# Two transformer-like blocks on one core: GpSimd takes the cosine products and the sister convolution tile, TensorE takes split sums of squares and picked gate rows

## The chip, the cores and the metric

One Trainium2 chip, one of its cores. The metric is the device time of one execution in microseconds (us); lower is better. Five engines work side by side: TensorE (PE; its weight loads are shown apart as PEld), VectorE (DVE), ScalarE (ACT), GpSimd (POOL) and SyncE (SP, which here issues the weight loads from memory).

## The reference

The program runs two blocks one behind the other, each with two layers (DEPTH = 2), on 512 tokens of width 1024, all in float32. What matters here:

```python
def first_block(x, ...):
    for i in range(DEPTH):
        h = rms_norm(x, attn_norm_g[i])
        proj = h @ w_in[i]
        q, k, v, u, vv = jnp.split(proj, split_at, axis=-1)
        q = rms_norm(q.reshape(b, s, N_HEADS, HEAD_DIM), q_norm_g[i])
        k = rms_norm(k.reshape(b, s, N_KV_HEADS, HEAD_DIM), k_norm_g[i])
        q = axial_rope(q, tables)          # q * cos - swapped(q) * sin
        k = axial_rope(k, tables)
        attn_o = gqa_attention(q, k, v)
        sg_o = spatial_gating(jax.nn.gelu(u), jax.nn.gelu(vv), ...)   # rms_norm over heads of 64 first
        ...
def second_block(x, ...):
    for i in range(DEPTH):
        z = rms_norm_2(x, attn_pre_norm[i]) @ w_in[i]
        aq, ak, av, conv_u, gdn_qkv, gdn_gate, gdn_a, gdn_b = jnp.split(z, offsets, axis=-1)
        y_attn = dilated_attention_mixer(aq, ak, av, positions)
        y_conv = conformer_conv_mixer(conv_u, ...)     # causal depthwise convolution, 31 taps, 256 channels
        y_gdn = gated_deltanet_mixer(gdn_qkv, ...)     # g: decay per token and head, beta: gate per token and head
        x = x + rms_norm_2(mix @ w_out[i], attn_post_norm[i])
        ...
```

In the delta rule the decay between two tokens of a chunk is exp(G[a] - G[b]), with G the running sum of g in the chunk.

## The kernel before

Activations lie transposed: features on 128 partitions, 512 tokens along the row. Every matrix product is made of **units**: one unit is an output tile of 128 features x 512 tokens. A weight tile of 8 x 128 x 128 is loaded into `raw`, ACT rounds it to fp32r (`whi`, `hi_next`, L1564), DVE makes the rest (`wlo = raw - whi`, `low`, L2276), and PE forms 24 products in fp32r (`whi` with `h_hi`, `whi` with `h_lo`, `wlo` with `h_hi`; L701). The weights are double buffered and units use two accumulator banks, `ACC`; unit i + 2 waits for the `low` that DVE issues in its own step i, and for the copy out of its bank. An ordinary float32 product on PE shows as two records in the trace.

Each engine's program is an unrolled list whose steps carry the number i of the unit: PE runs unit i and then small work of step i; ACT and DVE begin their step i when unit i is done. Engines meet only in semaphores, and nothing reorders an engine's queue.

**Block 1, input units (i = 0 to 13).** Tiles: v, k, four of q, four of vv, four of u. For k and q (j = 0 to 4), in DVE's steps: the copy out of the bank (L2377); then `qk_norm` (scale by the root of the mean square, L2331), `qk_rotary` (product with the sine table, a shuffle of lanes, product with the cosine table, subtraction; L2337 to L2343) and `qk_low`. ACT squares the tile into `msq` (`qk_square`), PE sums over the 64 features of a head with a float32 product with the block matrix `blk` (`head_sums`, L874, behind unit j + 2), and ACT takes log and exp of it (`qk_rs`). The four vv tiles go the same way behind units 10 and 11 (`gated_sums`, L883).

**Block 2, input units (i = 0 to 23, "input stage").** Beside them run the rotary of the four attention tiles (its sine part on POOL, L660), the scores of four heads (`scores`, L1127; DVE's `row_max`, L2666, must have read the bank before the next, semaphore `S_used`), `scores_turned` (L1142), `exponentials` on ACT, the products with counts on POOL (`counted`, L635), `probs_values` (L1164), the short convolutions of the delta rule (`short_taps`, L2687), and the 31-tap convolution of two tiles: taps 0 to 22 of both tiles on DVE (`taps`, L2710, in steps 9 to 20 by the list `beside`), the last 8 of tile 0 on DVE (`late_tap`, L2796), the last 8 of tile 1, the **sister tile**, as a product on ACT (`tap_product`, L2017) that POOL adds (L676).

The gates' running sums are made behind unit 20 (`decay_sums`). Behind units 20 to 23 PE runs `head_in(h)`, h = 0 to 3 (the text calls these steps heads 0 to 3; the trace shows them after the last products of units 20 to 23): a row of decays, broadcast to all partitions, by four products of a broadcast column of g with the triangle `tri` (L1197), the same for beta with the identity (L1203), then the transposes of k (L1210, waits for `turned_used`: ACT has read the former head's bank) and of v (L1214, waits for ACT's `short_silu`). ACT's `head_scaled(h)` uses them and ends with L1943.

**Levels.** Behind the units come 24 steps n of a blockwise inversion, with three groups of 16 short PE records each (`level_first` L1305, `level_second` L1327, `level_turned` L1348). ACT copies each turned result to `xd` (L2033, `xt_kept`); `level_first(n)` waits for the copy of step n - 4. ACT's late tap products stand in the same list, each waiting until POOL has freed one of two buffers.

## Time and profile before

| | |
|---|---|
| median of 3 runs | 2551.18 us (2549.28 to 2551.55) |
| the profiled execution, its own time | 2552.15 us |
| span of its instructions | 2550.4 us |
| mean granted TensorE clock | 0.995 |
| busy, share of the span | PE 98%, PEld 78%, DVE 61%, ACT 43%, POOL 9% |
| block 1's two input stages | about 36 to 116 us and 590 to 669 us |
| block 2's two input stages | about 1132 to 1347 us and 1837 to 2052 us |

The span is the time from the first to the last instruction; the execution's own time lies 1.75 us above it. A record of a pipelined product lasts longer than the distance to the next one, so the pace of products is read from their starts or ends, not from their durations. "Idle before" names who ended an engine's wait.

### The profile page before, as it was taken

How to read it: one execution, taken by the hardware profiler on the slowest of the kernel's cores; microseconds unless marked ns; L12 is line 12 of the kernel's file. 1: busy time of each engine (PE TensorE's matmuls, PEld its weight loads, DVE VectorE, ACT ScalarE, POOL GpSimd, SP SyncE). 2: the span in 40 equal slices, each digit the busy share in tenths (PEclk: the TensorE clock that was granted, in tenths of full speed). 3: DMA queues.
4: the chain of work that ended last, by engine and by line, in shares of the span. 5: the costliest groups of instructions: out<-in, count | busy, mean ns of one | idle time of the engine just before them, and what ended most of it. 6: DMA issues, size and time to landing. Idle time of an engine off the chain costs nothing.

```text
span 2550.4 us, 36617 instructions
## 1 busy us (share of the span) xinstructions
PE 2492.4 (98%) x12846; PEld 1992.5 (78%) x12856; DVE 1545.0 (61%) x1994; ACT 1094.3 (43%) x1597; POOL 227.2 (9%) x186
## 2 busy tenths in 40 slices
PE   7999999999999999999999999999999999999998
PEld 5768888887668888887688778888776887788886
DVE  5766755757666736647986554344579865643444
ACT  4655423435554424433485442233334754431323
POOL 1010000000000000004212020000142120200000
PEclk9999999999999999999999999999999999999999
DMA  4203332333113333342120223233222202233333
GB/s 134 78 17 91 95 109 84 100 98 88 58 42 99 97 96 96 103 111 74 50 75 11 66 83 107 86 96 97 80 72 58 67 19 65 77 107 90 96 97 95
DMA packets 384483, 208.07 MB, mean 82 GB/s; under 512 B 9866, under 2 KB 380500, under 8 KB 384372
## 3 DMA queue, kind: packets, MB, share of 16 engines
q1 hardware_dynamic: 381284, 202.79, 27.5%
q0 software_dynamic: 2176, 3.06, 0.6%
q8 instruction: 65, 1.06, 0.2%
q10 hardware_dynamic: 912, 0.77, 0.1%
q14 instruction: 46, 0.38, 0.0%
HBM read 205.34 MB, written 2.10 MB: 81 GB/s over the span
## 4 chain that ended last, share of the span: by engine, by line
PE 88%; DVE 7%; ACT 2%; issue 1%; DMA 0%; POOL 0%; DVEq 0%; SPq 0%; ACTq 0%; POOLq 0%
PE ps L701 64%; PE ps L720 6%; PE ps L986 2%; DVE yc L2710 1%; DVE wlo L2276 1%; ACT whi L1564 1%; PE ps L1305 1%; PE ps L1164 1%; PE ps L1046 1%; PE ps L1048 1%; PE ps L1047 1%; PE ps L1176 1%; PE ps L1426 1%; PE ps L1428 1%; PE ps L1427 1%
## 5 line engine op out<-in xcount | busy, mean ns | idle before, releaser
L1564 ACT ACTIVATE whi<-raw 128x1024 fp32r<-128x1024 f32 (+1 forms) x354 | 395.8, 1118 | 989.4 <-PE ps L701 844.2
L701 PE MATMUL ps<-h_hi,whi 128*128 128x512 f32 x1920 | 761.8, 397 | 2.3 <-DVE za L2616 1.7
L701 PE MATMUL ps<-h_lo,whi 128*128 128x512 f32 x1920 | 750.0, 391 | 0.0
L701 PE MATMUL ps<-h_hi,wlo 128*128 128x512 f32 x1920 | 513.3, 389 | 0.0
L2276 DVE TENSOR_TENSOR wlo<-raw,whi 128x1024 fp32r<-128x1024 f32 (+1 forms) x354 | 467.0, 1320 | 64.2 <-ACT whi L1564 63.0
L701 PEld LDWEIGHTS ps<-h_hi,whi 128*128 128x128 f32 x1920 | 362.2, 189 | 84.3 <-issue 4.2
L701 PEld LDWEIGHTS ps<-h_lo,whi 128*128 128x128 f32 x1920 | 362.1, 189 | 78.7 <-issue 4.3
L701 PEld LDWEIGHTS ps<-h_hi,wlo 128*128 128x128 f32 x1920 | 360.5, 188 | 74.9
L701 PE MATMUL ps<-a_hi,whi 128*128 128x512 f32 x592 | 230.3, 389 | 0.0
L701 PE MATMUL ps<-a_lo,whi 128*128 128x512 f32 x592 | 230.3, 389 | 0.0
L3039 DVE TENSOR_TENSOR cv<-ps,rstd 128x512 f32<-128x512 f32 x80 | 55.3, 692 | 228.7 <-PE ps L701 228.7
L701 PE MATMUL ps<-a_hi,wlo 128*128 128x512 f32 x592 | 152.4, 389 | 0.0
L2525 DVE TENSOR_TENSOR pad<-ps,rstd 128x512 f32<-128x512 f32 x88 | 61.0, 693 | 130.6 <-PE ps L701 118.4
L701 PEld LDWEIGHTS ps<-a_lo,whi 128*128 128x128 f32 x592 | 111.1, 188 | 23.1
L701 PEld LDWEIGHTS ps<-a_hi,wlo 128*128 128x128 f32 x592 | 111.1, 188 | 23.0
L701 PEld LDWEIGHTS ps<-a_hi,whi 128*128 128x128 f32 x592 | 111.1, 188 | 23.0
L2488 DVE TENSOR_TENSOR x_sb<-x_sb,ps 128x512 f32 (+1 forms) x40 | 27.5, 687 | 110.1 <-PE ps L701 94.2
L2534 DVE SCALAR_TENSOR_TENSOR cv<-pad,pc,cv 128x512 f32<-128x512 f32 x88 | 66.1, 751 | 11.0
L1815 ACT ACTIVATE cv<-pad,pc,pb 128x512 f32<-128x512 f32 x88 | 70.6, 802 | 0.1
L2965 DVE COPY y_sb<-ps 128x512 f32<-128x512 f32 (+1 forms) x24 | 16.6, 691 | 88.8 <-PE ps L701 66.6
L1827 ACT ACTIVATE a_hi<-prod 128x512 f32 (+1 forms) x44 | 27.9, 633 | 97.8 <-DVE prod L2541 97.8
L2710 DVE SCALAR_TENSOR_TENSOR yc<-ypad,pd,yc 128x512 f32<-128x512 f32 x88 | 68.5, 819 | 1.6
(429 smaller groups left out, 3427.0 us busy)
## 6 DMA issues: line engine op xcount, KB each, us to landing
raw<-in_w_up SPq DMA_DIRECT2D x128, 512.0 KB, 3.8
raw<-in_w_down SPq DMA_DIRECT2D x64, 704.0 KB, 4.5
raw<-in_w_in SPq DMA_DIRECT2D x82, 512.0 KB, 3.8
raw<-in_w_gate SPq DMA_DIRECT2D x40, 512.0 KB, 3.8
raw<-in_w_o SPq DMA_DIRECT2D x16, 512.0 KB, 3.6
raw<-in_w_out SPq DMA_DIRECT2D x16, 512.0 KB, 3.7
xs<-in_x SPq DMA_DIRECT2D x2, 1024.0 KB, 6.8
raw<-in_w_gate SPq DMA_DIRECT2D x8, 256.0 KB, 2.8
```

Of the source, the lines that this page charges most:

```text
L701: return pe.matmul(ps[:, ACC[s], :], w[s][:, k, :], r[:, k, :], start=start, stop=stop)
L720: return pe.matmul(ps[:, ACC[s], :], w[s][:, k, :], r[:, k, :], start=start, stop=stop)
L986: pe.matmul(ps[:, TRN[h % 2], :], vaug[:, h // GROUP, h % 2, kt, :], probs[:, kt, :], start=(kt == 0), stop=(kt == TB - 1)).then_inc(PV_do ...
L1564: act.activation(whi[s][:, 0:kt, :], raw[s][:, 0:kt, :], ACT.Copy).then_inc(w_hi_ready.sem, 1)
L1815: act.activation(cv[s][:], pad[s][:, 1:SEQ + 1], ACT.Identity, scale=param(pb, L, 2 * NF + col), bias=param(pc, L, 2 * NF + col))\
L1827: act.activation(tile(a_hi, j), prod[:], ACT.Copy).then_inc(ahi_ready.sem, 1)
L2276: dve.tensor_tensor(wlo[s][:, 0:kt, :], raw[s][:, 0:kt, :], whi[s][:, 0:kt, :].bitcast(F32), ALU.subtract).then_inc(w_lo_ready.sem, 1)
L2488: dve.tensor_tensor(tile(x, n), tile(x, n), ps[:, ACC[s], :], ALU.add).then_inc(acc_free.sem, 1)
L2525: dve.tensor_tensor(pad[s][:, 1:SEQ + 1], ps[:, ACC[s], :], rstd[:], ALU.mult).then_inc(acc_free.sem, 1)
L2534: dve.scalar_tensor_tensor(cv[s][:], pad[s][:, 2:SEQ + 2], param(pc, L, col), cv[s][:], ALU.mult, ALU.add)\
L2710: ins = dve.scalar_tensor_tensor(yc[:, t, :], src, w, yc[:, t, :], ALU.mult, ALU.add)
L3039: dve.tensor_tensor(cv[s][:], ps[:, ACC[s], :], rstd[:], ALU.mult).then_inc(acc_free.sem, 1)
```

## The change

1. **Sums of squares in two parts (block 1).** POOL rounds each square tile to fp32r (`sq_hi`) and takes the rest (`sq_lo`); PE sums both with `blk_r`, an fp32r copy of `blk`: two fp32r products in place of one float32 product, 9 tiles in each layer. The sums come one unit later (behind unit j + 3), in four banks instead of two; `qk_rs`, `qk_norm`, `qk_rotary`, `qk_low` and `qk_high` move one step later with them.
2. **Cosines on POOL (block 1).** POOL makes the product with the cosine table; DVE keeps sine product, shuffle and subtraction.
3. **Sister tile off DVE (block 2).** All 31 taps of tile 1 are products on ACT that POOL adds: by the table `SIDE`, taps 0 to 15 in steps 10 to 17, taps 16 to 19 in steps 18 to 21, taps 20 to 30 in the levels. DVE keeps tile 0.
4. **Picked gate rows (block 2).** `decay_sums` moves from behind unit 20 to behind unit 12. DVE splits the running sums and beta into fp32r parts (`gate_split`), PE turns them behind unit 13 (four transposes), DVE keeps the rows (`gate_rows`), and `head_in` picks a head's row with one fp32r product of 512 columns for the decays and one for beta, instead of four float32 products of 128 columns each.
5. Two unused tables are no longer loaded.

```diff
--- before.py
+++ after.py
+    SIDE = {**{10 + p: (2 * p, 2 * p + 1) for p in range(8)}, **{18 + n: (16 + n,) for n in range(4)}}
+    SIDE_IN = 20
...
+                def square_split(j):
+
+                    if j <= NQ:
+                        pool.wait_ge(qksq_ready.sem, qksq_ready.at(L, j))
+                    else:
+                        pool.wait_ge(vvsq_ready.sem, vvsq_ready.at(L, j - NQ - 1))
+                    if j >= 4:
+                        pool.wait_ge(qkstat_ready.sem, qkstat_ready.at(L, j - 4))
+                    square = msq[:, j % 2 if j <= NQ else (j - NQ - 1) % 2, :]
+                    nc.gpsimd.tensor_copy(sq_hi[:, j % 4, :], square).then_inc(sq_split.sem, 1)
+                    pool.wait_ge(sq_split.sem, sq_split.at(L, 2 * j))
+                    nc.gpsimd.tensor_tensor(sq_lo[:, j % 4, :], square, sq_hi[:, j % 4, :].bitcast(F32), ALU.subtract).then_inc(sq_split.sem, 1)
+                    pool.wait_ge(sq_split.sem, sq_split.at(L, 2 * j + 1))
+
+                def cosines(i):
+
+                    pool.wait_ge(qkn_ready.sem, qkn_ready.at(L, i))
+                    if i >= 2:
+                        pool.wait_ge(rope_ready.sem, rope_ready.at(L, i - 2))
+                    nc.gpsimd.tensor_tensor(probs[:, 2 + i % 2, :], zk[:] if i == 0 else zq[:, i - 1, :], rope[:, 0, :], ALU.mult)\
+                        .then_inc(cos_ready.sem, 1)
+                    pool.wait_ge(cos_ready.sem, cos_ready.at(L, i))
+
+                for j in range(NQ + 1):
+                    square_split(j)
+                    if j >= 2:
+                        cosines(j - 2)
+                for i in range(NQ - 1, NQ + 1):
+                    cosines(i)
...
+                    if h == 1:
+                        pool.wait_ge(qm_ready.sem, qm_ready.at(L, h))
+                        for j in range(NQ + 1, NQ + 1 + NS):
+                            square_split(j)
...
+                def side_tap(k):
+
+                    pool.wait_ge(tap_scaled.sem, tap_scaled.at(L, k))
+                    if k > 0:
+                        if k > 1:
+                            pool.wait_ge(late_tapped.sem, late_tapped.at(L, k - 2))
+                        nc.gpsimd.tensor_tensor(yc[:, 1, :], yc[:, 1, :], msq2[:, k % 2, :], ALU.add)\
+                            .then_inc((late_tapped if k < CT - 1 else dw_ready).sem, 1)
+
+                for i in range(10, 22):
+                    p = i - 10
+                    if p < 2 * AH:
+                        for kt in range(2 * (p % 2), 2 * (p % 2) + 2):
+                            counted(p // 2, kt)
+                    for k in SIDE[i]:
+                        side_tap(k)
...
-                for n in range(CT - TAPS_IN):
-                    pool.wait_ge(tap_scaled.sem, tap_scaled.at(L, n))
-                    if n >= 1:
-                        pool.wait_ge(late_tapped.sem, late_tapped.at(L, n - 1))
-                    nc.gpsimd.tensor_tensor(yc[:, 1, :], yc[:, 1, :], kb[:, n % 2, :], ALU.add)\
-                        .then_inc((late_tapped if n < CT - TAPS_IN - 1 else dw_ready).sem, 1)
+                for k in range(SIDE_IN, CT):
+                    side_tap(k)
...
-                def head_sums(i):
-
-                    pe.wait_ge(qksq_ready.sem, qksq_ready.at(L, i))
-                    if i == 0:
+                def square_sums(j):
+
+                    bank = ps[:, (STAT + ROT)[j % 4], :]
+                    pe.wait_ge(sq_split.sem, sq_split.at(L, 2 * j + 1))
+                    if j == 0:
                         pe.wait_ge(rstd_ready.sem, rstd_ready.at(L * 2, 0))
-                    if i >= 2:
-                        pe.wait_ge(qkrs_ready.sem, qkrs_ready.at(L, i - 2))
-                    pe.matmul(ps[:, STAT[i % 2], :], blk[:], msq[:, i % 2, :], start=True, stop=True).then_inc(qkstat_ready.sem, 1)
-
-                def gated_sums(t):
-
...
-                    pe.matmul(ps[:, STAT[t % 2], :], blk[:], msq[:, t % 2, :], start=True, stop=True).then_inc(vvstat_ready.sem, 1)
+                        pe.wait_ge(acc_free.sem, V * 2 + 3)
+                    if 4 <= j < NQ + 5:
+                        pe.wait_ge(qkrs_ready.sem, qkrs_ready.at(L, j - 4))
+                    pe.matmul(bank, blk_r[:], sq_hi[:, j % 4, :], start=True, stop=False)
+                    pe.matmul(bank, blk_r[:], sq_lo[:, j % 4, :], start=False, stop=True)\
+                        .then_inc((qkstat_ready if j <= NQ else vvstat_ready).sem, 1)
...
                     unit(V + i // 2, i % 2, KD, h_hi, h_lo, need_h(L * 2))
-                    if i - 2 <= NQ:
-                        head_sums(i - 2)
+                    if 0 <= i - 3 <= NQ:
+                        square_sums(i - 3)
                     if i == 4:
                         turn_spatial()
                     if i == 6:
                         turn_values()
                     if i in (10, 11):
-                        gated_sums(2 * i - 20)
-                        gated_sums(2 * i - 19)
+                        square_sums(NQ + 1 + 2 * i - 20)
+                        square_sums(NQ + 1 + 2 * i - 19)
...
+                def turn_gate_parts():
+
+                    pe.wait_ge(gate_parts.sem, gate_parts.at(L, 0))
+                    for tb in range(TB):
+                        mm = pe.transpose(ps[0:4 * GH, TRN[1], tb * P:(tb + 1) * P], gate_split[:, tb, :].bitcast(F32), ident[:])
+                    mm.then_inc(gate_turned.sem, 1)
...
-                        mm = pe.matmul(ps[:, ROT[0], tb * P:(tb + 1) * P], cols["g"][:, tb, h:h + 1].to_broadcast([P, P]),
-                                       tri[:], start=True, stop=True)
-                    mm.then_inc(grow_ready.sem, 1)
+                    n = 4 * GH
+                    pe.matmul(ps[:, ROT[0], :], gate_pick[0:n, h:h + 1].to_broadcast([n, P]), gate_rows[0:n, :],
+                              start=True, stop=True).then_inc(grow_ready.sem, 1)
                     if h >= 1:
                         pe.wait_ge(kb_ready.sem, kb_ready.at(L, h - 1))
-                    for tb in range(TB):
-                        mm = pe.matmul(ps[:, ROT[1], tb * P:(tb + 1) * P], cols["beta"][:, tb, h:h + 1].to_broadcast([P, P]),
-                                       ident[:], start=True, stop=True)
-                    mm.then_inc(brow_ready.sem, 1)
+                    pe.matmul(ps[:, ROT[1], :], gate_pick[0:n, GH + h:GH + h + 1].to_broadcast([n, P]), gate_rows[0:n, :],
+                              start=True, stop=True).then_inc(brow_ready.sem, 1)
...
+                    if i == 12:
+                        decay_sums()
+                    if i == 13:
+                        turn_gate_parts()
...
+                def tap_product(k):
+
+                    if k == 0:
+                        act.wait_ge(glu_ready.sem, glu_ready.at(L, 1))
+                        dst, bias = yc[:, 1, :], param(pd, L, D_BIAS + 1)
+                    else:
+                        dst, bias = msq2[:, k % 2, :], 0.0
+                    if k >= 3:
+                        act.wait_ge(late_tapped.sem, late_tapped.at(L, k - 3))
+                    order.told(act.activation(dst, ypad[:, 1, k:k + SEQ], ACT.Identity, bias=bias, scale=param(pd, L, D_DW + k * NC + 1)),
+                               tap_scaled, L, k)
...
+                    for k in SIDE.get(i, ()):
+                        tap_product(k)
...
-                    if n in (0, 1):
-                        act.wait_ge(kk_ready.sem, kk_ready.at(L, GH - 2 + n))
-                        tap_product(n)
-                    if 2 <= n - 2 < CT - TAPS_IN:
-                        act.wait_ge(late_tapped.sem, late_tapped.at(L, n - 4))
-                        tap_product(n - 2)
+                    if n < CT - SIDE_IN:
+                        tap_product(SIDE_IN + n)
...
-                    order.step(dve.tensor_tensor(t1[:], z, rope[:, 0, :], ALU.mult))
-                    order.settle()
-                    order.told(dve.tensor_tensor(z, t1[:], t2[:], ALU.subtract), rope_ready, L, i)
+                    dve.wait_ge(cos_ready.sem, cos_ready.at(L, i))
+                    order.told(dve.tensor_tensor(z, probs[:, 2 + i % 2, :], t2[:], ALU.subtract), rope_ready, L, i)
...
+                def decay_columns():
+
+                    dve.wait_ge(G_ready.sem, G_ready.at(L, 0))
+                    order.told(dve.tensor_copy(flat("gc"), ps[:, TRN[1], 0:NCOL]), gc_kept, L, 0)
+                    order.settle()
+                    order.told(dve.tensor_tensor(flat("dg"), ps[:, TRN[1], NCOL:2 * NCOL], flat("gc"), ALU.subtract), dg_ready, L, 0)
+                    for n, name in enumerate(("gc", "beta")):
+                        order.step(dve.tensor_copy(gate_split[:, :, 2 * n * GH:(2 * n + 1) * GH], cols[name][:]))
+                    order.settle()
+                    for n, name in enumerate(("gc", "beta")):
+                        hi, lo = (slice((2 * n + e) * GH, (2 * n + e + 1) * GH) for e in range(2))
+                        ins = dve.tensor_tensor(gate_split[:, :, lo], cols[name][:], gate_split[:, :, hi].bitcast(F32), ALU.subtract)
+                        if n == 0:
+                            order.step(ins)
+                        else:
+                            order.told(ins, gate_parts, L, 0)
...
+                        w, src = param(pd, L, D_DW + k * NC), ypad[:, 0, k:k + SEQ]
+                        if k == 0:
+                            ins = dve.tensor_scalar(yc[:, 0, :], src, w, param(pd, L, D_BIAS), ALU.mult, ALU.add)
+                        else:
+                            ins = dve.scalar_tensor_tensor(yc[:, 0, :], src, w, yc[:, 0, :], ALU.mult, ALU.add)
+                        order.step(ins)
...
+                    if i == 12:
+                        decay_columns()
+                    if i == 13:
+
+                        dve.wait_ge(gate_turned.sem, gate_turned.at(L, 0))
+                        order.told(dve.tensor_copy(gate_rows[0:4 * GH, :], ps[0:4 * GH, TRN[1], :]), rows_kept, L, 0)
```

On PE, at head 1 of block 2 (ps is PSUM; `tri` and `ident` are constants, `col_g` and `col_beta` the gates by token), the program before has:

```order
L1197 MATMUL ps<-tri,col_g 128x128 [waits eg_ready]
L1197 MATMUL ps<-tri,col_g 128x128 x3
L1203 MATMUL ps<-ident,col_beta 128x128 [waits kb_ready]
L1203 MATMUL ps<-ident,col_beta 128x128 x3
L1210 MATMUL ps<-ident,gk 128x128 [waits l2n,turned_used]
```

and the changed one, at the same place:

```order
L1253 MATMUL ps<-gate_rows,gate_pick 128x512 [waits eg_ready]
L1257 MATMUL ps<-gate_rows,gate_pick 128x512 [waits kb_ready]
L1263 MATMUL ps<-ident,gk 128x128 [waits l2n,turned_used]
L1263 MATMUL ps<-ident,gk 128x128 x3
L1267 MATMUL ps<-ident,gv 128x128 [waits sc_silu]
```

The eight short products have become two; the waits behind them stay as they were.

On ACT, at the start of the levels (`gk<-ps` is the copy to `xd`, `kb<-ypad` or `sqt<-ypad` a tap product; the semaphore that the tap products wait for is named after its first use and is POOL's count of added taps), before:

```order
L1948 ACTIVATE eg_last<-eg 128x4
L2017 ACTIVATE kb<-ypad,pd 128x512 [waits kk_ready] x2
L2033 ACTIVATE gk<-ps 128x256 [waits osq_ready] x3
L2017 ACTIVATE kb<-ypad,pd 128x512 [waits qkstat_ready]
L2033 ACTIVATE gk<-ps 128x256 [waits osq_ready]
```

and in the changed program:

```order
L2012 ACTIVATE eg_last<-eg 128x4
L1955 ACTIVATE sqt<-ypad,pd 128x512 [waits qkstat_ready] x2
L2094 ACTIVATE gk<-ps 128x256 [waits osq_ready]
L1955 ACTIVATE sqt<-ypad,pd 128x512 [waits qkstat_ready]
L2094 ACTIVATE gk<-ps 128x256 [waits osq_ready]
```

The first tap product that waits for POOL stood behind three copies and now stands behind one.

On POOL, in block 1's input stage, before, the queue went from the loads of tables straight to the query copies:

```order
L555 DMA sgb<-in_sg_b 64x4x128 x2
L564 COPY qm<-qab 64x512 [waits qr_ready] x2
L564 COPY qm<-qab 64x512 [waits ST_ready,qr_ready] x2
L574 TENSOR_TENSOR ssq<-sqt 128x512 [waits osq_ready,qm_ready]
L574 TENSOR_TENSOR ssq<-ssq,sqt 128x512 [waits osq_used,osq_ready] x2
```

and in the changed program splits and cosine products stand between them:

```order
L597 CAST sq_hi<-sqt 128x512 [waits qksq_ready,sq_split]
L599 TENSOR_TENSOR sq_lo<-sqt,sq_hi 128x512 [waits sq_split]
L607 TENSOR_TENSOR probs<-zk,rope 128x512 [waits qkn_ready,sq_split]
L597 CAST sq_hi<-sqt 128x512 [waits qksq_ready,cos_ready]
L599 TENSOR_TENSOR sq_lo<-sqt,sq_hi 128x512 [waits sq_split]
```

POOL's work here is 5 splits with 5 cosine products, and 4 more splits for vv behind the first two query copies.

## Rows read from the trace of the kernel before

**Rows 1.** The page: busy time, share of the span and instructions of each engine.

```profile
PE 2492.4 (98%) x12846; PEld 1992.5 (78%) x12856; DVE 1545.0 (61%) x1994; ACT 1094.3 (43%) x1597; POOL 227.2 (9%) x186
```

**Rows 2.** Waits of PE: who for whom, us in total, times, longest.

```profile
PE ps L1127 <- DVE mx L2666: 5.9, 3, 2.8
```

**Rows 3.** Timeline of PE around two square sums: start us, us, instruction, count.

```profile
89.75 1.75 PE L701 MATMUL ps<-h_hi,wlo 128*128 128x512 f32 x7
...
91.79 0.39 PE L701 MATMUL ps<-h_hi,wlo 128*128 128x512 f32 x1
92.02 1.88 PE L883 MATMUL ps<-sqt,blk 128*128 128x512 f32 x4
```

**Rows 4.** Timeline of PE, block 2, heads 0 and 1.

```profile
1313.24 1.05 PE L1197 MATMUL ps<-tri,col_g 128*128 128x128 f32 x8
1314.12 1.06 PE L1203 MATMUL ps<-ident,col_beta 128*128 128x128 f32 x8
1315.02 0.60 PE L1210 MATMUL ps<-ident,gk 128*128 128x128 f32 x4
1315.45 0.60 PE L1214 MATMUL ps<-ident,gv 128*128 128x128 f32 x4
...
1324.94 0.60 PE L1210 MATMUL ps<-ident,gk 128*128 128x128 f32 x4
```

**Rows 5.** Windows of block 2's step 11, of step 13, and layer 2's step 11.

```profile
core 0: us, PE busy (x) PEld busy (x) DVE busy (x) ACT busy (x) POOL busy (x), PEclk, DMA share, GB/s
1214.34:1228.24 13.90, 10.83 (x36) 8.12 (x37) 13.44 (x17) 3.31 (x8) 2.07 (x2) 0.75 0.14 38
1239.12:1246.88 7.76, 7.69 (x36) 6.11 (x37) 7.41 (x10) 1.84 (x4) 1.51 (x2) 1.00 0.24 67
1920.12:1932.50 12.38, 9.31 (x36) 7.18 (x37) 11.92 (x16) 3.31 (x8) 2.07 (x2) 0.86 0.16 42
```

**Rows 6.** Timeline of PE in step 11: the wait.

```profile
1218.08 1.22 PE L1127 MATMUL ps<-qkr 64*128 64x512 f32 x2 [2.83 <-DVE mx L2666]
```

**Rows 7.** Timeline of DVE, block 2's input stage.

```profile
1175.23 1.77 DVE L2658 TENSOR_TENSOR tb<-za,rope 128x512 f32<-128x512 f32 x1
...
1182.23 0.68 DVE L2658 TENSOR_TENSOR tb<-za,rope 128x512 f32<-128x512 f32 x1
...
1207.56 5.77 DVE L2710 SCALAR_TENSOR_TENSOR yc<-ypad,pd,yc 128x512 f32<-128x512 f32 x6
...
1277.68 1.42 DVE L2710 SCALAR_TENSOR_TENSOR yc<-ypad,pd,yc 128x512 f32<-128x512 f32 x2
```

**Rows 8.** Timeline of POOL, the input stage and the levels.

```profile
1171.23 10.00 POOL L660 TENSOR_TENSOR probs<-za,rope 32x512 f32<-32x512 f32 x6
...
1209.56 2.56 POOL L635 TENSOR_TENSOR probs<-probs,times 128x512 f32<-128x512 f32 x2 [28.34 <-ACT probs L1892]
...
1357.13 11.43 POOL L676 TENSOR_TENSOR yc<-yc,kb 128x512 f32<-128x512 f32 x8
```

**Rows 9.** Timeline of DVE in block 1: its steps 6 and 7 begin.

```profile
70.18 0.68 DVE L2377 TENSOR_TENSOR vv<-ps,rstd 128x512 f32<-128x512 f32 x1
...
77.08 0.68 DVE L2377 TENSOR_TENSOR vv<-ps,rstd 128x512 f32<-128x512 f32 x1
```

**Rows 10.** Timeline of ACT at heads 0 and 1.

```profile
1314.15 1.67 ACT L1919 ACTIVATE gv<-gv 128x512 f32<-128x512 f32 x3
...
1322.80 1.19 ACT L1943 ACTIVATE vb<-ps,col_beta 128x128 f32<-128x128 f32 x4
```

**Rows 11.** Timeline of DVE at head 3: the mask of head 2.

```profile
1346.11 0.87 DVE L2754 TENSOR_TENSOR gk<-gv,lev 64x256 f32<-64x256 f32 x2
```

**Rows 12.** Timeline of PE: behind head 3, and `level_first(5)`.

```profile
1347.34 0.68 PE L1243 MATMUL ps<-ident,gk 64*64 64x64 f32 x16
...
1357.47 0.66 PE L1305 MATMUL ps<-gk,gv 64*64 64x64 f32 x16
```

**Rows 13.** Timeline of ACT in the levels: copy of step 1, third tap product.

```profile
1356.31 0.39 ACT L2033 ACTIVATE gk<-ps 128x256 f32<-128x256 f32 x1 [1.64 <-PE ps L1348]
...
1358.44 0.72 ACT L2017 ACTIVATE kb<-ypad,pd 128x512 f32<-128x512 f32 x1 [0.35 <-POOL yc L676]
```

115 lines of the change are left out of this document (48 added, 67 removed).

## The prediction

> **What bounds the kernel now.** First the busy table of the page: PE is busy 98% of the span and DVE 61%; ACT and POOL lie far below [rows 1]. A change therefore pays where it takes products from PE's path or ends one of its waits, and costs where it makes a new wait of PE. Then the list of PE's waits: the one wait of size that the change touches is `scores` waiting for DVE's `row_max`, 5.9 us in three places, the longest 2.8 [rows 2]. So I add up PE's path piece by piece and ask at each place whether the helper engines keep up. The sum is made against the profiled execution's own 2552.15 us (span 2550.4 and 1.75 around it); the median of the runs is 0.97 lower, and I subtract that at the end.
>
> **Part 1, sums of squares.** Products in fp32r stand back to back, so the price is the distance between starts: seven starts begin at 89.75, the next single record at 91.79, the float32 sums at 92.02. One fp32r product of 512 columns is thus about 0.227 us (1.75 - 0.39 over six distances). The last of these records ends at 92.02 + 1.88 = 93.90, the product before ends at 92.18: 1.72 for two float32 sums, 0.86 each [rows 3]. Two fp32r products are 0.45. Saved 0.41 in 9 tiles of 2 layers: **-7.3**.
>
> **Part 4, picked rows.** In a head the decays start at 1313.24, beta at 1314.12, the transposes of k at 1315.02 and of v at 1315.45 [rows 4]: 0.88 and 0.90 for four float32 products of 128 columns, 0.43 for four transposes. One fp32r product of 512 columns is 0.23, so 0.65 is saved each; 2 rows in 4 heads of 2 layers: **-10.5**. The added transposes behind unit 13 are +0.45 in each layer: **+0.9**. `decay_sums` only moves.
>
> **Part 3, step 11 of block 2.** Step 11 takes 13.90 us at a granted clock of 0.75, an undisturbed step (13) 7.76 at 1.00, layer 2's step 11 12.38 at 0.86 [rows 5]. The excess is 6.1 and 4.6, together 10.8: the wait, 2.83 us at 1218.08 [rows 6], and the stretch at the lower of TensorE's two clocks (1.2 instead of 2.4 GHz) that follows it. DVE is late because in step 10 it makes six taps in 5.77 us, three of them the sister's [rows 7]. Without those three it gains about 2.9, which alone covers 2.83, and step 9 loses sister taps too, about 1.9 more. POOL has only one add by then. `row_max` should come about 2 us before PE asks. Wait and slow stretch go: **-10.8**.
>
> What POOL's new work costs DVE is seen in two pairs of rows. A product with both inputs in SBUF takes 1.77 us at 1175.23 while POOL runs six products of its own (1171.23 to 1181.23), and 0.68 at 1182.23 when POOL is idle: 1.09 more. The six taps of 5.77 would be 4.3 at the 0.71 of the pair at 1277.68; they met two POOL products of 1.28 [rows 7, 8]: 1.5 us for two, 0.74 each. I take 0.74, since it is measured over whole POOL instructions, and keep 0 and 1.09 as ends (0: POOL's operation falls where DVE reads PSUM or waits). The trace does show that DVE instructions with an operand in PSUM keep their 0.68 [rows 9]. The Trainium skill (SBUF — State Buffer, "Who interferes with whom") says more: a DVE instruction with two SBUF inputs contends with a GpSimd instruction that reads SBUF, through a port pair that is an exclusive lock, while one with at most one SBUF input is spared. By that each of POOL's operations could cost DVE its full 1.28, where the taps show 0.74; so the rule speaks against this change, and is weighed again beside the last rival.
>
> In the input stage of block 2, DVE drops 23 taps of 0.71 in each layer (16.3 us) and pays for 19 added POOL operations at 0.74 (14.1): hardly lighter from step 12 on, and it receives the gate work. The split and the kept rows stand in its steps 12 to 14 ahead of what `probs_values` waits for. I give this 2 us of PE's time in each layer, an estimate that lies between nothing and the 2.83 of the old wait: **+4**.
>
> **Part 2 and the splits, block 1.** DVE drops 5 products of about 0.7 in a layer and meets 15 POOL operations in steps 2 to 7. It is already no faster than PE there: its steps 6 and 7 begin 6.90 us apart [rows 9], while 24 products of 0.227 and a sum of 0.86 make 6.3 on PE. In the two middle steps three POOL operations cost 2.2 and one product of 0.7 goes. The sums are needed one unit later, which gives the chain square, split, sum, log and exp the room of a unit. But the first vv split, about 2.5 us of POOL time from DVE's square, is late behind unit 10. I take 1.0 in each layer: **+2**, with 0 and the fourth case below as ends.
>
> **What the heads give back.** PE's heads become 1.3 us shorter, but what they wait for doesn't move.
> - Head 0 asks for the transposes of v 1.3 us earlier, at 1314.15. ACT's three `short_silu` start at 1314.15 and take 0.56 each, so the first ends at 1314.75 [rows 10]; ahead of them ACT has one more tap product (0.72) in that step. Ready at about 1315.6: +1.5.
> - Head 1 waits for `turned_used`, ACT's last read of head 0. ACT's group ends at 1322.80 + 1.19 = 1323.99 [rows 10], plus 0.7 for the added tap product of the step, less what it starts earlier; PE would ask at 1323.6, that is 1324.94 [rows 4] less 1.3: +0.9.
> - Head 3's follow-up needs DVE's mask of head 2, done at 1346.11 + 0.87 = 1346.98 [rows 11]. PE came at 1347.34 [rows 12], a slack of 0.36 against 1.3 saved: +0.95.
>
> Together 3.4 in each layer: **+6.8**. Step 19's sum of squares waits for ACT behind another added tap: **+0.6** in both layers.
>
> **The levels.** The third tap product now stands behind the first copy and waits for POOL to add the first late one. POOL comes to these adds only at 1357.13, behind its work for the last head, and runs them 1.43 apart [rows 8]. So ACT can go on at about 1358.5, makes the product (0.72), then the copy of step 1 (0.39). That copy stood at 1356.31 [rows 13]; now it ends at about 1359.5. `level_first(5)`, at 1357.47 [rows 12], needs it: +2.0. Steps of PE follow 1.4 apart against POOL's 1.43: +0.2. DVE's last `low` meets more POOL work: +0.6. In each layer 2.8: **+5.6**. Eleven adds end at 1357.13 + 11 x 1.43 = 1372.9, in time for the mean of the shifted levels.
>
> **Sum:** -7.3 - 10.5 + 0.9 - 10.8 + 4 + 2 + 6.8 + 0.6 + 5.6 = -8.7. The execution becomes 2543.4, the median about 2542.4. The two table loads lie beside the start of the program: nothing.
>
> **The rivals.** A median below 2546.1 is faster and above 2556.3 slower, by 0.2%, which is about what a measurement of this kernel can tell from no change.
>
> - **Forecast (0.45): -8.7**, 2542.4. Its own range, with the unknown costs (+4, +2) between 0 and twice their size: 2537 to 2548.
> - **The give-backs hide (0.25).** ACT is busy for only 1.84 of the 7.76 us of step 13 [rows 5], and an engine that PE reaches earlier may itself have started earlier. Of the added waits only the levels' is then left, since POOL's start at 1357.13 hangs on the last head and not on these engines. -27.7 + 5.6 is -22; with the levels' wait halved -25: **2526 to 2530**. Against it: head 0 and head 3 have slacks of 0 and 0.36 in rows.
> - **The gain is handed back (0.18).** DVE doesn't lead in step 11, because POOL's adds and products there cost it 1.09 instead of 0.74; some of the wait stays, and with it the slow stretch, 5 us of the 10.8. Or the 2 us wait in the levels is followed by a stretch at the lower clock, as the wait of 2.83 was: with 1.7 us a layer (12.38 us at a clock of 0.86 lose 0.14 of them) that is +3.4. Either leaves **2546 to 2551**, the same or barely faster.
> - **Slower (0.12): DVE loses the port to POOL.** In block 1, 15 POOL operations at 0.9, between 0.74 and 1.09, cost DVE 13.5 us a layer and 3.5 are taken away: +10 in stretches where it already lags by 0.6 a step; I let PE see 5.5 of it. In block 2 the 19 adds at 0.9 cost 17.1 against 16.3 removed, so DVE stays late and the 10.8 are not won, with the 5 us of the other side. -8.7 + 2 x 4.5 + 10.8 = +11, less about 4 of the given-back terms, which a late DVE hides: +7, **2558**. It decides where PE's new waits are 7 us a layer above the forecast's (13.8 from -8.7 to +5.1). The Trainium skill (SBUF — State Buffer, "Who interferes with whom") has this as its rule; at the full 1.28 of each operation, an estimate in the same way gives about 2580, and the 0.74 of the taps speaks against it.
>
> **How the numbers follow.** Faster: the forecast nearly whole (0.42 of 0.45), the second case 0.25, a little of the third (0.03): 0.70. Same: 0.18. Slower: 0.12. The range leaves out the lower half of the second case and the far side of the last: 2529 to 2555.
>
> **What the changed profile would show.** Right: square sums as pairs of records 0.23 apart; heads starting with two 512-column products; step 11 at about 7.8 to 9 us with the clock at 1.00 and no wait for `mx`; `turned_used` and `short_silu` among PE's waits at heads 0 and 1; a wait of about 2 us for ACT's `xt_kept` at `level_first(5)`, and ACT waiting there for POOL's add. Wrong would make it: waits for `sq_split` or `rope` in block 1 beyond 1 us a layer, DVE's taps above 1 us each throughout, a stretch of clock below 1.00 in the levels, or no waits at all at the heads.

## The result, and the profile after

The changed kernel takes 2564.28 us (median of 5 runs, 2562.71 to 2564.70) against 2551.26 us for the kernel before in the same session (2549.28 to 2551.55): a ratio of 1.0051, with a 95% interval of 1.0038 to 1.0064. It is 13.0 us slower, where 8.7 us less had been forecast.

The busy times answer to [rows 1]: PE's fell by 2 us, POOL's rose by 132 us, and the span grew by 12.2 us. The work went away as planned, and PE stood still or ran slowly for longer than that.

```profile
PE 2490.3 (97%) x12742; PEld 1986.7 (78%) x12752; DVE 1541.7 (60%) x1951; ACT 1121.7 (44%) x1643; POOL 359.7 (14%) x275
```

PE's list of waits (us in total, times, longest) answers to [rows 2]. The wait for `mx` in step 11 is gone, and new ones stand in the list, of which these are the largest: the split of the gates, ACT's copy in the levels, the split squares and the spatial weights in block 1, ACT's `za` (made from a sum of squares by log and exp) at head 0, and POOL's last add ahead of the convolution's mean in the levels.

```profile
PE ps L1240 <- DVE gate_split L2725: 4.5, 2, 2.3
PE ps L1360 <- ACT gk L2094: 4.0, 3, 1.9
...
PE ps L928 <- POOL sq_lo L599: 3.7, 2, 1.8
...
PE ps L1253 <- ACT za L1626: 3.2, 2, 1.6
...
PE ps L1413 <- POOL yc L714: 1.9, 2, 0.9
PE ps L945 <- ACT wT L1728: 1.8, 2, 0.9
```

Block 2 has 26 input units (i = 0 to 25), as its program shows (`N_IN2` is 3 x 2 + 2 x 2 + 4 x 4), so the heads stand behind units 22 to 25 and not 20 to 23; "step i" below runs from the end of unit i to the end of unit i + 1. The tap products of `SIDE` end in step 21, the step ahead of head 0.

Windows of the changed kernel, cut at the ends of units, answer to [rows 5]: block 1 behind unit 10, step 11, step 13 in both layers, and steps 21 and 22 around head 0.

```profile
core 0: us, PE busy (x) PEld busy (x) DVE busy (x) ACT busy (x) POOL busy (x), PEclk, DMA share, GB/s
91.55:101.63 10.08, 8.23 (x30) 6.32 (x29) 5.94 (x5) 5.50 (x7) 7.51 (x6) 0.83 0.43 132
...
1216.71:1224.52 7.81, 7.74 (x39) 6.19 (x39) 7.39 (x10) 4.54 (x10) 3.95 (x5) 1.00 0.24 67
...
1235.48:1251.61 16.13, 13.63 (x44) 10.40 (x46) 11.45 (x18) 3.55 (x6) 6.44 (x5) 0.68 0.24 65
1945.93:1961.93 16.00, 13.50 (x44) 10.22 (x46) 11.45 (x18) 3.55 (x6) 6.30 (x5) 0.68 0.25 66
1312.36:1330.18 17.82, 15.54 (x61) 12.20 (x60) 14.24 (x19) 16.73 (x35) 1.29 (x1) 0.81 0.31 88
```

Step 11 is as forecast: 7.81 us at a clock of 1.00. (The margin is smaller than forecast: DVE's row maximum ends at 1216.94 and PE asks for it at 1217.32, 0.4 us later and not 2.) Step 13 took 8.5 us before (1238.53 to 1247.05; 9.0 in layer 2) and takes 16.1 now, at a mean clock of 0.68. PE's timeline shows why: the transposes of the split wait 2.26 us for DVE, and the products behind them come 0.43 apart instead of 0.227 until about 1248 (TensorE at 1.2 instead of 2.4 GHz).

```profile
1237.74 0.90 PE L1240 MATMUL ps<-ident,gate_split 128*16 128x128 f32 x4 [2.26 <-DVE gate_split L2725]
...
1244.49 0.63 PE L753 MATMUL ps<-h_lo,whi 128*128 128x512 f32 x1
1244.92 0.63 PE L753 MATMUL ps<-h_hi,whi 128*128 128x512 f32 x1
...
1248.49 0.39 PE L753 MATMUL ps<-h_lo,whi 128*128 128x512 f32 x1
1248.72 0.39 PE L753 MATMUL ps<-h_hi,whi 128*128 128x512 f32 x1
```

On DVE, the same stretch (L2765 is the short convolution, L2333 `low`): three short taps take 3.65 us and `low` 2.31, where the taps of step 13 take 2.33 and its `low` 1.22. POOL makes two products and two adds beside the first group. Beside the second taps it is idle, and its next product starts 0.03 us after the second `low` has started.

```profile
1230.27 3.65 DVE L2765 SCALAR_TENSOR_TENSOR gq<-zp,pd,gq 128x512 f32<-128x512 f32 x3
1233.85 2.31 DVE L2333 TENSOR_TENSOR wlo<-raw,whi 128x1024 fp32r<-128x1024 f32 x1
...
1236.37 0.94 DVE L2721 CAST gate_split<-col_gc 128x16 fp32r<-128x16 f32 x1
...
1237.51 0.17 DVE L2725 TENSOR_TENSOR gate_split<-col_beta,gate_split 128x16 fp32r<-128x16 f32 x1
...
1242.28 2.33 DVE L2765 SCALAR_TENSOR_TENSOR gq<-zp,pd,gq 128x512 f32<-128x512 f32 x3
1244.52 1.22 DVE L2333 TENSOR_TENSOR wlo<-raw,whi 128x1024 fp32r<-128x1024 f32 x1
```

The kernel before has the products with counts beside its step 12 as well, and its three short taps were slow already; what is new there is the slow `low` (1.21 us before) and a cast of 16 columns that takes 0.94 us, where it takes 0.17 in the kernels without adds in that place (quiet12, no_side). From the kernel before:

```profile
1232.86 3.77 DVE L2687 SCALAR_TENSOR_TENSOR gq<-zp,pd,gq 128x512 f32<-128x512 f32 x3
1236.55 1.21 DVE L2276 TENSOR_TENSOR wlo<-raw,whi 128x1024 fp32r<-128x1024 f32 x1
```

DVE also enters step 12 late: its step 11 takes from 1217.78 to 1227.90, 10.1 us, where PE's now takes 7.81.

POOL's timeline: the same pair of products takes 1.54 us in step 11 and 2.11 us behind the `low` of 1244.52. There it is POOL that was held up. Its two adds of step 12 end at 1237.28; the cast that began at 1236.37 ends at 1237.31.

```profile
1220.67 1.54 POOL L678 TENSOR_TENSOR probs<-probs,times 128x256 f32<-128x256 f32 x2 [3.71 <-ACT probs L1944]
...
1233.34 3.94 POOL L714 TENSOR_TENSOR yc<-yc,sqt 128x512 f32<-128x512 f32 x2
1244.55 2.11 POOL L678 TENSOR_TENSOR probs<-probs,times 128x256 f32<-128x256 f32 x2 [7.27 <-ACT probs L1944]
```

**Where the time went.** The end of each unit's last product was read in both traces; the difference, stage by stage and over both layers, against the terms of the forecast:

| stage | forecast | measured | of it lost to the clock |
|---|---|---|---|
| block 1's input stages | -5.3 | +1.7 | 1.7 |
| step 11 | -10.8 | -10.9 | (5.2 won back) |
| steps 12 and 13 | +4.9 | +16.3 | 10.3 |
| steps 14 to 19 | +0.6 | +0.6 | 0 |
| heads, levels | +1.9 | +6.3 | 3.4 |

(The loss to the clock is the window's length times one minus its mean clock: 16.13 x 0.32 = 5.2, for instance. Not in the table: the start of the program, -0.6, step 10, -0.6, and the end, -0.5. Block 1's +1.7 is all in layer 1, where the slow stretch is. The measured +6.3 of the last row is +2.0 in the heads and +4.4 in the levels. All of this is one profiled execution of each kernel.)

### The profile page after: what moved, and what is told of

Same layout as the page of the kernel before. It is cut to its first block, busy times and chain, and to the rows that moved or that the text cites. A ratio compares the mean times of both kernels' runs of the same rounds, so it can differ in the third digit from the quotient of the medians.

```text
span 2562.6 us, 36582 instructions
## 1 busy us (share of the span) xinstructions
PE 2490.3 (97%) x12742; PEld 1986.7 (78%) x12752; DVE 1541.7 (60%) x1951; ACT 1121.7 (44%) x1643; POOL 359.7 (14%) x275
## 4 chain that ended last, share of the span: by engine, by line
PE 80%; DVE 10%; ACT 5%; issue 3%; POOL 2%; DMA 0%; DVEq 0%; SPq 0%; ACTq 0%; POOLq 0%
PE ps L753 60%; PE ps L772 6%; DVE wlo L2333 2%; PE ps L1033 1%; POOL yc L714 1%; ACT whi L1619 1%; DVE gq L2765 1%; DVE yc L2786 1%; PE ps L1093 1%; PE ps L1095 1%; PE ps L1094 1%; DVE gv L2765 1%; PE ps L1483 1%; PE ps L1482 1%; PE ps L1481 1%
## 5 line engine op out<-in xcount | busy, mean ns | idle before, releaser
L2333 DVE TENSOR_TENSOR wlo<-raw,whi 128x1024 fp32r<-128x1024 f32 (+1 forms) x354 | 485.4, 1372 | 63.9 <-ACT whi L1619 62.8
L714 POOL TENSOR_TENSOR yc<-yc,sqt 128x512 f32<-128x512 f32 x60 | 89.3, 1489 | 51.6 <-ACT sqt L1955 46.7
L645 POOL TENSOR_TENSOR h_lo<-pad,h_hi 128x512 fp32r<-128x512 f32 x9 | 14.6, 1620 | 476.8 <-ACT h_hi L2229 476.8
```

The source lines that it names most:

```text
L714: nc.gpsimd.tensor_tensor(yc[:, 1, :], yc[:, 1, :], msq2[:, k % 2, :], ALU.add)\
L2333: dve.tensor_tensor(wlo[s][:, 0:kt, :], raw[s][:, 0:kt, :], whi[s][:, 0:kt, :].bitcast(F32), ALU.subtract).then_inc(w_lo_ready.sem, 1)
```

## The experiments

Each ran against the kernel before on the same chip. "Place" and "backlog" are two theories of step 13: that the split only stands too late in DVE's queue, or that DVE as a whole has no room there.

One thing bears on all differences of a few us below. Behind the same wait of 2.26 us in step 13 the slow stretch isn't always the same: in the ten layers of five kernels that have this wait (the change, no_block1, levels, vv_later, cos_dve), step 13 lasts about 16.1 us three times, 14.5 five times (mean clock 0.76 to 0.77) and 11.4 twice (clock 1.00).

**gates_early.** DVE's gate work ahead of its taps.

```diff
+                    if i == 12:
+                        decay_columns()
                     if 9 <= i < 9 + len(beside):
...
-                    if i == 12:
-                        decay_columns()
                     if i == 13:
```

> The change, with DVE's gate work (the copies of the running sums and their split) in step 12 ahead of its taps instead of behind its rounding rest of the weights. Theory A (place): PE waits 2.3 us for the split behind unit 13 only because the split stands behind 2.3 us of low and a late short convolution; moved forward it is ready 3 us before PE asks, the wait and the stretch of 10.24 us at half clock go in both layers: 7.4 us each, about 2549 to 2551. Theory B (backlog): DVE is late in steps 12 and 13 as a whole, since POOL's adds slow it; the wait only moves on to DVE's next result, the row maximum of step 13, 1 to 2 us with a stretch at half clock behind it: 2558 to 2564.

2562.61 us, ratio 1.0042 (1.0028 to 1.0055). The wait for the split is gone and two others have come: 1.50 for the row maximum, and 2.45 for the kept rows ahead of step 14's products. The place was not the cause.

```profile
1236.81 0.73 PE L1174 MATMUL ps<-qkr 64*128 64x512 f32 x2 [1.50 <-DVE mx L2744]
...
1246.50 3.31 PE L1213 MATMUL ps<-probs,vaug 128*128 128x512 f32 x4 [2.45 <-DVE gate_rows L2918]
```

**no_rows, no_side, no_block1.** The change without part 4, without part 3, without parts 1 and 2: the code of before at these places.

> The change without its part 4 (gate rows by float32 products as before, running sums behind unit 20). Theory A: the step behind unit 13 gives back 7.3 us in each layer and the heads cost about what they cost before, 2547 to 2550. Theory B: PE waits for DVE's row maximum in step 13 instead, with half clock behind it: 2553 to 2558. My prediction's view that part 4 is a gain of 2 to 3 us in all would give 2567.

> The change without its part 3 (sister tile's taps on DVE as before, last eight by ACT and POOL). Theory A: step 11 costs its 10.8 us again, the levels give back 2.1 and head 0 about 1 in each layer, the split behind unit 13 is still late by about 1 us and the clock falls behind it: 2560 to 2566. Theory B: with POOL quiet DVE makes its low in 1.22 us, the split is in time, 14.6 us go and 10.8 come back: 2551 to 2556.

> The change without its parts 1 and 2 (block 1 as before). The trace says that block 1's two stages are 1.4 and 0.4 us longer after the change, all of the 7.3 us saved on PE given back in waits: 2561 to 2563. The rival, that the sums in two parts are a net gain that other stages hide: 2567 to 2570.

no_rows: 2558.24 us, 1.0024 (1.0014 to 1.0035). no_side: 2554.66 us, 1.0013 (1.0004 to 1.0023). no_block1: 2558.38 us, 1.0027 (1.0017 to 1.0036). Each part taken away makes the changed kernel faster, by 6.0, 9.6 and 5.9 us; that is 21.5 for a loss of 13, since two parts share a wait. Of no_block1's 5.9, more than its expectation had, some 3 us are step 13 with its shorter slow stretches (14.5 us in both layers instead of 16.1 and 16.0), so they say nothing of block 1.

Without the rows, step 13 has only a wait of 0.35 us, for the row maximum, so the backlog alone hardly stops PE there: it takes the gate work on top. (A wait of 1.3 us for ACT in step 19 is new in that run.) Without the side tile PE waits 0.9 us for the split in one layer and 1.4 for the kept rows, and step 11's 2.8 us wait is back. Head 0's wait for `za` stays without the rows (1.5 us) and goes without the side tile: the sister tile's work made it, not PE's shorter heads.

**light12, quiet12.** Two ways to give DVE room: fewer taps of its own in steps 12 and 13, or POOL nearly quiet beside them.

```diff
-    beside = [3, 3, 3, 2, 2, 2, 2, 2, 1, 1, 1, 1]
+    beside = [3, 3, 3, 0, 0, 3, 3, 3, 2, 1, 1, 1]
```

> The change, with DVE's taps of its own tile taken out of steps 12 and 13 (3,3,3,0,0,3,3,3,2,1,1,1 a step instead of 3,3,3,2,2,2,2,2,1,1,1,1). After the first four runs the theory is: DVE has no room in steps 12 and 13 for the gate work (about 1.8 and 0.7 us) on top of what POOL's adds cost it. Then 1.5 us less in step 12 ends most of the 2.3 us wait for the split, no new wait for the row maximum or the kept rows comes, and the half clock behind it goes: 5 to 7 us in each layer, 2550 to 2555. Rival: the load only moves to steps 14 to 16, whose three taps beside POOL's adds make PE wait there: 2560 to 2565.

```diff
-    SIDE = {**{10 + p: (2 * p, 2 * p + 1) for p in range(8)}, **{18 + n: (16 + n,) for n in range(4)}}
+    COUNTS = [2, 1, 0, 1, 3, 2, 2, 2, 2, 2, 1, 1]
+    SIDE = {10 + p: tuple(range(sum(COUNTS[:p]), sum(COUNTS[:p + 1]))) for p in range(12)}
...
```

(with the later products in the levels as in the next experiment but one, and the mean one step later)

> The change, with the sister's products and adds at 2,1,0,1,3,2,2,2,2,2,1,1 in steps 10 to 21 (twelve in the levels, behind the copies, the mean one step later), so that POOL is nearly quiet in steps 11 to 13 while DVE's own work there stays. If the port is what makes the split late: low takes 1.2 us instead of 2.3 there, the wait behind unit 13 is under 0.5 us and no stretch at half clock follows. If it is the amount of DVE's own work, the wait stays above 1.5 us. The whole time says little, since ACT gets more to do in step 14: 2552 to 2562.

light12: 2558.38 us, 1.0026 (1.0015 to 1.0036), between the two forecasts. The wait for the split falls from 2.3 to 1.6 us, and no stretch at half clock follows: step 13 takes 10.66 us. quiet12: 2556.31 us, 1.0022 (1.0012 to 1.0031). The wait is gone, with DVE's own work unchanged: the window of step 13 in both layers has a clock of 1.00 and PE busy throughout.

```profile
1234.83:1243.83 9.00, 9.00 (x45) 6.79 (x43) 8.55 (x9) 2.87 (x5) 3.50 (x3) 1.00 0.23 59
1940.84:1949.84 9.00, 9.00 (x45) 6.78 (x42) 8.55 (x9) 2.87 (x5) 3.51 (x3) 1.00 0.22 58
```

DVE's `low` of step 12 still takes 1.94 us, beside the two products with counts, more than the 1.2 expected. But the `low` of step 11 takes 1.21 us instead of 2.29, the short taps of step 12 3.11 instead of 3.65, and the cast of the split 0.17 instead of 0.94: 2.8 us less for three adds fewer, and the split is ready before PE asks. Head 0 then waits 2.6 us for ACT and the mean 2.4 us for POOL, which is why the whole gains only 8 us.

**filled.** Products that nobody needs where PE waited for the split.

```diff
                     if i == 13:
+                        pe.wait_ge(acc_free.sem, (V + 7) * 2 + 1)
+                        for n in range(9):
+                            pe.matmul(ps[:, ACC[0], :], negones[:], h_hi[:, 0, :], start=True, stop=True)
                         turn_gate_parts()
```

> The change, with nine products of 512 columns into unit 14's bank, which nobody reads, right ahead of the transposes of the split: they fill about 2.0 of the 2.3 us that PE waits there. If the 10.24 us at half clock follow from PE standing still, the clock stays at 1.00 and about 5 us in each layer go although work was added: 2554 to 2557. If they come from something else (the transposes, the load of the step), nothing changes: 2563 to 2566.

2559.39 us, 1.0031 (1.0021 to 1.0042): 4.9 us less than the change with more work on PE, not the 7 to 10 expected. The wait is 0.25 us and the clock 1.00 in both layers' step 13, which takes 11.4 us instead of 16; the kept rows then make PE wait 1.9 us in step 14, which had been hidden.

```profile
1235.90 2.20 PE L1313 MATMUL ps<-h_hi,negones 128*128 128x512 f32 x9
1238.35 0.60 PE L1240 MATMUL ps<-ident,gate_split 128*16 128x128 f32 x4 [0.25 <-DVE gate_split L2728]
```

```profile
1236.06:1247.45 11.39, 11.07 (x52) 8.22 (x52) 10.76 (x16) 3.49 (x6) 6.77 (x5) 1.00 0.17 46
1943.10:1954.46 11.36, 11.05 (x52) 8.22 (x52) 10.73 (x16) 3.48 (x6) 6.75 (x5) 1.00 0.18 46
```

The trace of filled alone isn't proof: layer 2 of levels, with the same 2.26 us unfilled, has no slow stretch either and is as long.

```profile
1946.09:1957.46 11.37, 9.03 (x44) 6.88 (x44) 10.74 (x16) 3.48 (x6) 6.76 (x5) 1.00 0.17 46
```

What speaks for the connection is that eight of ten layers with the open wait have a slow stretch and neither of filled's has, and that filled's eight executions have mean clocks of 0.993 to 0.999 against 0.990 to 0.994 in the change's five.

**levels.** Products of the sister tile two a step in steps 10 to 20, none in 21; in the levels as before the change.

```diff
-    SIDE = {**{10 + p: (2 * p, 2 * p + 1) for p in range(8)}, **{18 + n: (16 + n,) for n in range(4)}}
-    SIDE_IN = 20
+    SIDE = {**{10 + p: (2 * p, 2 * p + 1) for p in range(11)}, 21: ()}
+    SIDE_IN = 22
...
-                    if n < CT - SIDE_IN:
+                    if n < 2:
                         tap_product(SIDE_IN + n)
+                    if 2 <= n - 2 < CT - SIDE_IN:
+                        tap_product(SIDE_IN + n - 2)
```

> The change, with tap products of the sister tile placed otherwise: two in each of steps 10 to 20, none in step 21, and in the levels two ahead of the copies and the third at step 4, as before the change. If the levels' wait comes from the third product standing behind the first copy, the 2.1 us of each layer and the 0.95 us in front of the mean go, and head 0 asks ACT about 0.7 us earlier in each layer: 6 to 9 us in all, 2555 to 2558. Rival: steps 18 to 20, with a second product each, give it back: 2562 to 2566.

2562.34 us, 1.0046 (1.0032 to 1.0059), within the spread of the change. The levels' wait of 1.9 us is gone and they are 2.4 us shorter in each layer, but head 0 waits 3.1 us for ACT's `za` instead of 1.6, although step 21 has no product. The trace shows the way: POOL's two adds of step 20 (1312.35 to 1315.95) hold up DVE, whose `low` takes 2.32 us and whose next two instructions 2.38 instead of 1.28, so that the copy ACT needs in step 21 comes late.

```profile
1312.48 2.32 DVE L2335 TENSOR_TENSOR wlo<-raw,whi 128x1024 fp32r<-128x1024 f32 x1
1314.72 2.38 DVE L2794 SCALAR_TENSOR_TENSOR gq<-gq,za 128x512 f32<-128x512 f32 x2
```

```profile
1317.93 0.72 ACT L2020 ACTIVATE gv<-zp,pd 128x512 f32<-128x512 f32 x1 [1.19 <-DVE zp L2679]
```

**vv_later, cos_dve.** Block 1: the second vv sum behind unit 11 (`{10: (0,), 11: (1, 2, 3)}` for the sums behind units 10 and 11, `vv_rs(1)` in ACT's step 11); and the cosine products back on DVE.

> The change, with the sum of squares of the second vv tile behind unit 11 instead of unit 10 (and its log and exp in ACT's step 11). If the split's lateness is the whole of block 1's loss there, 2.1 us go in each layer and the stretch of 3.4 us at half clock in layer 1: 5 to 6 us, 2558 to 2560. Rival: the later logs and exps make PE wait for the gated transposes behind unit 12: 2562 to 2566.

> The change, with block 1's cosine products back on DVE (POOL keeps the splits of the squares). Theory: a POOL operation costs DVE as much as the product of 0.69 us that it takes from it (0.74 in the rows of before), so nothing was won: the waits for low in block 1 stay about as they are, within 1.5 us of the change, 2562 to 2566. Rival, the port is the cause of block 1's waits: 2557 to 2561. Other rival, the move was worth its 0.69 a tile: 2567 to 2570.

vv_later: 2560.06 us, 1.0036 (1.0022 to 1.0049), 4.2 us less. The wait for the split square falls from 1.8 to 1.1 us a layer and the slow stretch behind it in layer 1 goes; 3.1 us of the trace's difference are again step 13 (14.5 us in both layers). cos_dve: 2561.87 us, 1.0043 (1.0029 to 1.0057), 2.4 us less with overlapping intervals. In its trace block 1's waits for `wT` (0.9) and for `sq_lo` (1.8) stand as they were: moving the cosines didn't cause them, and no gain from it can be measured.

**only_rows, taps_even.** The kernel before with part 4 alone, and with one line changed:

```diff
-    beside = [3, 3, 3, 2, 2, 2, 2, 2, 1, 1, 1, 1]
+    beside = [2, 2, 2, 2, 2, 2, 2, 2, 2, 2, 2, 1]
```

> The kernel before with part 4 alone (picked gate rows). If DVE's lack of room in steps 12 and 13 is there without any POOL work, PE waits about 1 us for the split and 1.4 us for the kept rows in each layer, some half clock behind them, against 10.5 saved and 0.9 added: 2546 to 2551. If POOL's adds alone made the split late: 2540 to 2543.

> The kernel before with one edit: the 23 taps that DVE makes of both tiles are spread 2,2,2,2,2,2,2,2,2,2,2,1 over steps 9 to 20 instead of 3,3,3,2,2,2,2,2,1,1,1,1. If step 11's wait is only a matter of when DVE makes its taps, two less in each of steps 9 and 10 (3 us) end it with the half clock behind it: 10.8 us less, 2540 to 2543, and the sister tile need not leave DVE. Rival: the taps moved to steps 12 to 19 make PE wait there: 2548 to 2554.

only_rows: 2551.40 us, 1.0004 (0.9995 to 1.0013), no difference; its heads are 2.2 us shorter in each layer, and the kept rows make PE wait 1.4 us. (In layer 2 the stretch behind step 11's old wait is also longer than before: step 11 takes 13.99 us against 12.48.) taps_even: 2542.63 us, **0.9965** (0.9952 to 0.9979). Step 11's wait was a matter of when DVE makes its taps; the sister tile need not leave DVE for it. The window of step 11 in both layers:

```profile
1213.32:1221.52 8.20, 8.01 (x37) 6.26 (x38) 7.82 (x11) 3.31 (x8) 2.07 (x2) 1.00 0.24 64
1913.99:1922.22 8.23, 8.04 (x37) 6.28 (x38) 7.85 (x11) 3.31 (x8) 2.07 (x2) 1.00 0.23 64
```

**combo.** The change with one own tap in steps 12 and 13, side counts 2,1,0,1,3,3,3,3,2,1,0,0, the levels as in levels, the mean a step later, vv_later's order.

> The change with what the first eight runs point to: DVE has one own tap in steps 12 and 13, the sister's products and adds are 2,1,0,1,3,3,3,3,2,1,0,0 in steps 10 to 21, the levels start their late products behind the copies with the mean one step later, and the second vv sum is behind unit 11. Expected: no wait for the split over 0.5 us, no 2 us wait in the levels, head 0 asks ACT for less: 15 to 20 us below the change, 2544 to 2550. Rival: three adds a step in steps 14 to 17 make DVE late there: 2552 to 2558.

2560.90 us, 1.0039 (1.0025 to 1.0052): a miss. Steps 12 and 13 have no wait, but ACT, not DVE, fell behind: its third product in a step waits for POOL's add, with everything behind it, and PE waits 5.9 us for ACT in front of the sums of squares of step 19, and 2.4 for POOL's last add in the levels.

```profile
1280.16 0.72 ACT L1955 ACTIVATE sqt<-ypad,pd 128x512 f32<-128x512 f32 x1 [2.86 <-POOL yc L715]
```

**rows_room, sums_room, both_room, rows_even, both_even.** Parts on the kernel before with spread taps (`beside` alone changes DVE's tap times; sums_room has taps_even's, the others those named below; split sums with vv_later's order, values turned behind unit 7, cosines on DVE).

> The kernel before, with part 4 (picked rows) and DVE's taps of both tiles at 2,2,2,1,1,2,2,2,2,2,3,2 in steps 9 to 20. The spread taps alone gave 2542.6. If the rows are worth what the heads show in the run of part 4 alone (2.2 us a layer) once DVE has room in steps 12 and 13: 2538 to 2541. Rival: the kept rows still hold PE up ahead of step 14's products, 2542 to 2546.

> The kernel before, with the taps spread evenly and part 1 (sums of squares in two parts), the second vv sum behind unit 11 and the values of block 1 turned behind unit 7 instead of 6 (so that they don't wait for ACT's copies of the spatial weights). If these were the places where the 7.3 us were lost: 4 to 6 us of them stay, 2537 to 2540. Rival: low of DVE is late by then as before and takes it back: 2541 to 2544.

> Both together: spread taps, picked rows, sums in two parts with the two later places. Sum of the two: 2533 to 2538, the fastest. Rival: one of the two hands its part back, 2539 to 2544.

> rows_room with the taps at 2,2,2,2,1,2,3,2,2,2,2,1 in steps 9 to 20. If the third tap of step 19 made head 0 wait: that wait (2.8 us and its half clock, 5 us a layer) goes, and the rows keep 2 us a layer: 2536 to 2540. If the wait belongs to the rows themselves: 2543 to 2547.

> rows_even with the split sums in their later places. The split sums gave nothing measurable on the spread taps (2541.0 against 2542.6), so this is within 2 us of rows_even: 2535 to 2540. Rival: 2543 to 2547 as above.

| | taps | us | ratio (95%) |
|---|---|---|---|
| rows_room | 2,2,2,1,1,2,2,2,2,2,3,2 | 2546.40 | 0.9985 (0.9976 to 0.9994) |
| sums_room | 2,2,2,2,2,2,2,2,2,2,2,1 | 2541.01 | 0.9966 (0.9952 to 0.9979) |
| both_room | as rows_room | 2546.64 | 0.9986 (0.9977 to 0.9995) |
| rows_even | 2,2,2,2,1,2,3,2,2,2,2,1 | 2539.40 | **0.9953** (0.9939 to 0.9966) |
| both_even | as rows_even | 2539.46 | 0.9956 (0.9942 to 0.9969) |

rows_room's wait of 2.8 us at head 0 comes from DVE's taps just ahead of it: ACT waits 2.17 and 2.46 us there for DVE's copies, and with one tap fewer in each of steps 19 and 20 the wait is not in rows_even's list. Which of the two taps did it wasn't separated. The largest waits in block 2's input stage that are left are these.

```profile
PE ps L1137 <- ACT qkr L1979: 3.5, 2, 1.8
...
PE ps L1203 <- DVE gate_split L2687: 1.8, 2, 0.9
```

The split sums add nothing that can be measured to any of the three bases (2541.01 against 2542.63, 2546.64 against 2546.40, 2539.46 against 2539.40): they save on PE and wait for DVE's `low` (1.5 us a layer) and for the split (1.1). The rows gain 3.2 us over taps_even, with overlapping intervals.

## Why the prediction was wrong

- **Step 11 (-10.8): right**, in size and cause; -10.9 in the trace.
- **The step that failed: "I give this 2 us of PE's time in each layer", steps 12 to 14.** The wait itself was right, 2.26 us against 2. What the term lacked was the slow stretch behind it, 5.2 and 5.1 us in the windows: steps 12 and 13 cost 16.3 us instead of 4.9. I had booked such a stretch as a gain in step 11, where a wait went, and not as a cost where waits came; only a rival had it, in the levels and at 1.7 us. With the wait filled (filled) or gone (quiet12, no_rows) the clock stays up in all six layers; with the wait open it falls in eight of ten. How long the stretch lasts isn't fixed by the wait: step 13 lost 5.2, 3.4 or 0 us to it in the kernels named above. Over all stages of the profiled execution the clock took 15.4 us that the sum didn't have, of the 21.7 between forecast and result.
- **The price of POOL's work (0.74 each): about right.** In step 12 four POOL operations cost DVE 1.3 in the short taps (3.65 against 2.33), 1.1 in `low` (2.31 against 1.22) and 0.8 in the cast (0.94 against 0.17): 3.2, or 0.8 each. The two products, and the slow taps beside them, were there before the change; its own three added adds of steps 11 and 12 cost 2.8 against quiet12, 0.9 each. The sum had this about right for a whole stage and didn't follow it step by step: DVE's step 11 lasts 10.1 us beside PE's 7.81.
- **Who is held up.** Instructions that read PSUM kept their times (row maximum 1.23 us at 1246.43, beside POOL). The prediction took this from [rows 9], where POOL is idle; other rows of the kernel before show it (0.69 us at 1171.81, beside POOL's products). The Trainium skill (SBUF — State Buffer, "Who interferes with whom") has this division, and says that the order of issue decides who is held up; the trace agrees with both: the second `low`, ahead of POOL, keeps its 1.22 and POOL pays, and the cast of 0.94 ends when POOL's add does. That cast has one SBUF input. The prediction left out that the section spares such instructions only outside the two-port modes, and names casts among those that can have one; which mode this cast ran in no row shows. The full 1.28 for each operation isn't seen. quiet12 shows that the adds make the split late, no_rows that without the gate work the delay is nearly harmless: both are needed.
- **The rival "slower" was nearest in time, but not in its account.** PE's losses are 10.9 us a layer above the forecast, beyond its mark of 7, but 7.7 of them came through the clock; step 11, which it held for lost, was won.
- **Block 1 (+2 against waits): mis-sized.** 7.3 us left PE and the stages are 1.7 longer, so 9.0 were lost, 1.7 of it to the clock. The rest is the late split that I named, 1.85 us in each layer instead of 1.0, and waits that I hadn't: PE, earlier by 0.4 a unit, meets ACT's copy of `wT` (0.9 us) and DVE's `low` (0.5). That DVE's products and the cosines balance was right (cos_dve).

```profile
90.98 0.61 POOL L597 CAST sq_hi<-sqt 128x512 fp32r<-128x512 f32 x1 [3.86 <-issue]
91.67 2.13 POOL L599 TENSOR_TENSOR sq_lo<-sqt,sq_hi 128x512 fp32r<-128x512 f32 x1
```

```profile
93.85 0.50 PE L928 MATMUL ps<-sq_hi,blk_r 128*128 128x512 f32 x1 [1.85 <-POOL sq_lo L599]
```

- **Heads (-10.5 + 6.8): near, for partly wrong reasons.** The prediction charged head 0 and head 1 with 0.7 each for an added tap product in their own steps. There is none: the heads stand behind units 22 to 25, and the last product is in step 21. The trace has a wait of 1.62 us at head 0 (forecast 1.5), but for `za` of step 21 and not for `short_silu`. Two things make `za` late: the product of step 21 (0.7), and DVE's copy, for which ACT waits, because POOL's add of step 20 (1310.65) has stretched `low` to 2.32 us. In layer 1 a stretch at half clock came behind it (0.81 over 17.82 us). ACT's last read of head 0 made PE wait 0.6 in one layer, where 0.9 in each was forecast.

```profile
1310.79 2.32 DVE L2333 TENSOR_TENSOR wlo<-raw,whi 128x1024 fp32r<-128x1024 f32 x1
```

```profile
1315.14 0.72 ACT L2020 ACTIVATE gv<-zp,pd 128x512 f32<-128x512 f32 x1 [0.71 <-DVE zp L2677]
```

- **Levels (+5.6, measured +4.4): right in the mechanism.** The third product waits for POOL, the copy behind it, and PE 1.90 us for the copy. The wait in front of the mean, which I had excluded, came too (0.95 us a layer): POOL's eleven adds take 16.25 us, 0.5 more than my pitch of 1.43 gives, and end later than PE asks. So the forecast's own terms were somewhat too high; for one of them, 0.6 for DVE's last `low`, no row was given and no run shows it.

```profile
1363.55 16.25 POOL L714 TENSOR_TENSOR yc<-yc,sqt 128x512 f32<-128x512 f32 x11
```

```profile
1364.85 0.72 ACT L1955 ACTIVATE sqt<-ypad,pd 128x512 f32<-128x512 f32 x1 [3.77 <-POOL yc L714]
1365.48 0.36 ACT L2094 ACTIVATE gk<-ps 128x256 f32<-128x256 f32 x1
```

```profile
1365.99 0.68 PE L1360 MATMUL ps<-gk,gv 64*64 64x64 f32 x16 [1.90 <-ACT gk L2094]
```

Still open: why a wait of about the same length has a slow stretch behind it in one layer or run and not in another. The change's head 0 has one in layer 1 alone, light12's 1.6 us in step 13 had none, and the 2.26 us of step 13 itself had none in layer 2 of levels and layer 1 of cos_dve. The 13.0 us are thus in part luck of the kernel's timing: with stretches as in no_block1 they would be about 3 fewer (an estimate from the windows of step 13).

## What to carry to other kernels

When a change takes a wait and a slow-clock stretch away, price every new wait of PE with such a stretch as well: here a 2.3 us wait cost 7.5 us, 5.7 in three sister kernels, and 2.3 where no stretch followed. Before moving work to another engine because its owner is late once, look at when the owner does it: one line of tap counts won 10 us in step 11 and kept 7.7, where moving the whole tile won 11 there and gave more back elsewhere. And an engine that is idle on average can be late just where the work is put: DVE and ACT ahead of head 0, POOL behind the last head. Look at the steps, not at the stage.

## What the runs showed of the hardware

- Behind a wait of PE of 2.26 us TensorE's granted clock fell from 1.00 (2.4 GHz) to half in eight of ten layers, with a mean of 0.68 or about 0.76 over the step. Nine added products of 512 columns in that wait made the kernel 4.9 us faster, with the clock at 1.00 in both layers.
- A DVE instruction of 1024 columns with both inputs in SBUF took 1.22 us alone, or when it began just ahead of POOL's work, and 2.3 us when it began behind a POOL add; a row maximum read from PSUM took 1.2 us either way. A cast of 16 columns with one SBUF input took 0.17 us alone and 0.94 us when it began beside a POOL add, ending when the add did (1237.31 and 1237.28).
